# First key tiles row by row from smaller first transfers, the first weight unit in halves, ten products over a zeroed tile ahead of them

## The reference, cut to what matters

```python
def reference(x, mem, ..., mem_2, ...):
    x = first_block(x, mem, ...)          # recurrences, cross attention over mem, feed-forward
    return second_block(x, mem_2, ...)    # two layers more

def cross_attention(h, m, w_q, w_kv, w_o):
    q = (h @ w_q).reshape(...)
    kv = m @ w_kv                         # m = rms_norm(mem, norm_mem_g)
    k = kv[..., :D_MODEL].reshape(...)
    ...
```

## Time and profile before

| | us |
|---|---|
| time, median of 3 runs | 2022.88 |
| lowest, highest | 2019.67, 2024.22 |
| span of the profiled execution | 2016.9 |
| TensorE busy in it | 1983.3 |
| first product of TensorE | 9.50 |
| head of w1 begins | 37.80 |

### The profile page before, as it was taken

The page is one execution under the profiler, slowest core; times in us unless marked ns, Lnnn a source line. Parts: engine busy times, 40 slices in busy tenths (PEclk is TensorE's granted clock), DMA queues, the critical chain, the costliest instruction groups (busy, mean ns, idle before and its releaser), DMA issues.

```text
span 2016.9 us, 37724 instructions
## 1 busy us (share of the span) xinstructions
PE 1983.3 (98%) x15408; PEld 1848.6 (92%) x15408; DVE 1341.4 (67%) x1866; ACT 1082.0 (54%) x1698; POOL 51.8 (3%) x47
## 2 busy tenths in 40 slices
PE   8999999999999999999999999999999999999998
PEld 8989988999899989899988998999899989888997
DVE  6786766787566667866767554655477677756554
ACT  5856555555454454556556444644454565645443
POOL 0021000000000000000100000000000001000000
PEclk9999999999999999999999999999999999999999
DMA  7522454666565547543564655565555535544553
GB/s 274 172 80 76 151 184 157 209 207 196 173 221 190 199 166 231 183 136 127 199 209 143 209 189 191 189 208 194 194 198 185 178 107 189 180 162 168 189 191 122
DMA packets 98730, 359.30 MB, mean 178 GB/s; under 512 B 11193, under 2 KB 11513, under 8 KB 98297
## 3 DMA queue, kind: packets, MB, share of 16 engines
q1 hardware_dynamic: 98560, 356.90, 52.4%
HBM read 353.65 MB, written 1.05 MB: 176 GB/s over the span
## 4 chain that ended last, share of the span: by engine, by line
PE 92%; ACT 3%; DVE 3%; issue 1%; DMA 0%; DVEq 0%; SPq 0%; ACTq 0%
PE ps L1039 17%; PE ps L1041 17%; PE ps L1040 17%; PE ps L1026 8%; PE ps L1115 7%; PE ps L1114 7%; PE ps L1113 7%; PE ps L1195 2%; PE ps L1080 2%; PE ps L1081 2%; PE ps L1082 2%; PE ps L1196 2%; PE ps L1202 2%; ACT whi L2462 1%; DVE wlo L1718 1%; ACT Xn L2466 1%
## 5 line engine op out<-in xcount | busy, mean ns | idle before, releaser
L1718 DVE TENSOR_TENSOR wlo<-raw,whi 128x1024 fp32r<-128x1024 f32 x635 | 773.1, 1227 | 462.4 <-ACT whi L2462 460.3
L2462 ACT ACTIVATE whi<-raw 128x1024 fp32r<-128x1024 f32 x635 | 664.6, 1056 | 353.8 <-PE ps L1115 154.4
L1039 PE MATMUL ps<-H,whi 128*128 128x256 f32 x2608 | 734.1, 281 | 2.5 <-DVE wlo L1718 1.8
L1040 PE MATMUL ps<-L,whi 128*128 128x256 f32 x2608 | 725.4, 278 | 0.0
L1041 PE MATMUL ps<-H,wlo 128*128 128x256 f32 x2608 | 725.4, 278 | 0.0
L1039 PEld LDWEIGHTS ps<-H,whi 128*128 128x128 f32 x2608 | 490.1, 188 | 8.5 <-issue 4.2
L1040 PEld LDWEIGHTS ps<-L,whi 128*128 128x128 f32 x2608 | 490.2, 188 | 0.6
L1041 PEld LDWEIGHTS ps<-H,wlo 128*128 128x128 f32 x2608 | 490.1, 188 | 0.0
L1113 PE MATMUL ps<-whi,HH 128*128 128x512 f32 x440 | 171.2, 389 | 0.0
L1114 PE MATMUL ps<-whi,HL 128*128 128x512 f32 x440 | 171.2, 389 | 0.0
L1115 PE MATMUL ps<-wlo,HH 128*128 128x512 f32 x440 | 171.2, 389 | 0.0
(11 more groups left out here) (439 smaller groups left out, 2938.6 us busy)
## 6 DMA issues: line engine op xcount, KB each, us to landing
raw<-in_ws SPq DMA_DIRECT2D x635, 512.0 KB, 3.8
prow<-in_rows SPq DMA_DIRECT2D x11, 512.0 KB, 5.8
row<-in_rows SPq DMA_DIRECT2D x9, 512.0 KB, 6.4
mema<-in_memT SPq DMA_DIRECT2D x4, 512.0 KB, 4.8
mema<-in_mem2T SPq DMA_DIRECT2D x4, 512.0 KB, 6.8
memb<-in_mem2T SPq DMA_DIRECT2D x4, 512.0 KB, 5.8
DT<-in_dec SPq DMA_DIRECT2D x2, 768.0 KB, 6.5
X<-in_x SPq DMA_DIRECT2D x1, 1024.0 KB, 10.7
```

Of the source, the lines that this page charges most:

```text
L1039: e.matmul(o, h, hs[k], start=first and k == 0, stop=False, skip_group_check=True)
L1040: e.matmul(o, h, ls[k], start=False, stop=False, skip_group_check=True)
L1718: e.tensor_tensor(m.wlo[:, n % SPL, :], r, h.bitcast(F32), SUB).then_inc(*c.lo.done(n))
L2462: e.activation(m.whi[:, n % SPL, :], m.raw[:, n % RAW, :], ACT.Copy).then_inc(*c.hi.done(n))
```

## The change

The first transfers become smaller and come in another order: a quarter of `mem`, the 8 columns of `vec` with its gain, the first half of weight unit 0, its second half, the next quarter, unit 1, two quarters, units 2 and 3; then the rest of `vec` in two pieces, and `cst`, X, unit 4 and `prow` as before. Unit 0 is split in two halves. Key tiles 0 to 3 are made together, two rows of `mem` at a time over all four tiles (`first_keys`), so that unit n holds rows 2n and 2n+1 of four tiles. GpSimd zeroes 256 columns of `rx`, and TensorE makes ten plain float32 products of 128 columns over them into a bank that nobody reads. Of the steps that follow, `keys` 4 and 5 now both stand ahead of `mem_added`, `keys_out` 0 to 2 and the transposes, `keys` 6 and 7 behind them; both `jn` stand behind all of key tiles 0 to 3.

```diff
@@ key_fillers
-        if n == 3 and i == 0:
-            steps += [("mem_added", 0)] + mem_sums(0) + [("keys_out", i, 0), ("keys_out", i, 1)]
-        elif n % 2 and (n > 3 or i):
+        if n % 2:
             steps.append(("keys_out", i, n // 2))
@@ order
     o.put("first")
-    for step in mem_pieces(0):
+    pieces = mem_pieces(0)
+    for step in pieces[:4]:
         o.put(*step)
-    o.fill.append(key_fillers(0)[1:])
-    o.work("keys", 0, 0)
+    for part, some in enumerate((pieces[4:6], pieces[6:7], pieces[7:], ())):
+        o.put("first_keys", part)
+        for step in some:
+            o.put(*step)
     o.put("jn", "x0", 0)
     o.put("jn", "x0", 1)
-    o.filler(4)
+    o.put("keys", 0, 4)
+    o.put("keys", 0, 5)
+    o.put("mem_added", 0)
+    for step in mem_sums(0):
+        o.put(*step)
+    for p in range(3):
+        o.put("keys_out", 0, p)
     for tb in range(2):
         o.put("jt", "x0", tb)
         o.put("jh", "x0", tb, 0)
         o.put("jh", "x0", tb, 1)
-    o.filler(10 ** 6)
+    o.put("keys", 0, 6)
+    o.put("keys", 0, 7)
+    o.put("keys_out", 0, 3)
@@ tensor_program
+    def first():
+        bank = bank_for("warm")
+        e.wait_ge(*pool.after("warm"))
+        for _ in range(WARM):          # 10
+            mm = e.matmul(bank[:, 0:128], m.rx[:, 0:128], m.rx[:, 128:256], start=True, stop=True, ...)
+        mm.then_inc(*pe.done(("warm",)))
+
+    def first_keys(part):
+        mem, mh, ml = m.mem(0)
+        if part == 0:
+            for j in range(2):
+                bank_for("keys", 0, j, hold=True)
+        for k in (2 * part, 2 * part + 1):
...
+            if part == 0:
+                e.wait_ge(*(c.hi.sem, 1) if k else act.after("first_hi"))
+            for n, i in rows:
...
+                e.matmul(o, m.weight(i)[0], mh[:, k, :], ...)
+            if part == 0:
+                e.wait_ge(*(c.lo.sem, 1) if k else dve.after("first_lo"))
+            for n, i in rows:
...
+                e.matmul(o, m.weight(i)[1], mh[:, k, :], ...)
+            e.wait_ge(*dve.after("ml", 0, k))
+            for n, i in rows:
...
+                mm = e.matmul(o, m.weight(i)[0], ml[:, k, :], ...)
@@ vector_program, mem; scalar_program the same with first_half, second_half and first_halves(p + 1)
                 if i == t == 0:
-                    remainders(1)
+                    first_remainder()
+                elif i == 0 and t == 1:
+                    second_remainder()
...
+        if i == 0 and p < 4:
+            remainders(p + 1)
         if i == 0 and p == 3:
-            remainders(3)
+            e.wait_ge(c.land["vec"], 32)
@@ pool_program, first
+        e.memset(m.rx[:, 0:256], 0.0).then_inc(*pool.done(("warm",)))
@@ sync_program, first
-        e.dma_start(m.vec[:, :], ins["vec"]).then_inc(c.land["vec"], 16)
-        memory(0, 0)
-        units(1)
-        memory(0, 1)
+        a = VEC_AT["norm_mem_g"][0]
+        first_memory(0)
+        e.dma_start(m.vec[:, a:a + 8], ins["vec"][:, a:a + 8]).then_inc(c.land["gain"], 16)
+        e.dma_start(m.raw[:, 0, 0:512], ins["ws"][0, :, 0:512]).then_inc(c.land["first"], 16)
+        e.dma_start(m.raw[:, 0, 512:1024], ins["ws"][0, :, 512:1024]).then_inc(c.land["raw", 0], 16)
+        loaded[0] = 1
+        first_memory(1)
+        units(2)
+        first_memory(2)
+        first_memory(3)
         units(4)
+        for to, of in ((0, a), (a + 8, NV)):
+            e.dma_start(m.vec[:, to:of], ins["vec"][:, to:of]).then_inc(c.land["vec"], 16)
```

More of the change, by code:

```diff
@@ L24 @@
 NU = 635
+WARM = 10
 C_W = math.exp(-0.5)
@@ L1265, in keys @@
              [dve.after("ml", i, t) for t in range(8)], quarters or (0, 4))
+    def first():
+        bank = bank_for("warm")
+        e.wait_ge(*pool.after("warm"))
+        for _ in range(WARM):
+            mm = e.matmul(bank[:, 0:128], m.rx[:, 0:128], m.rx[:, 128:256], start=True, stop=True, skip_group_check=True)
+        mm.then_inc(*pe.done(("warm",)))
[5 more added lines that the diff above has]
+        for k in (2 * part, 2 * part + 1):
+            rows = []
+            for n in range(4):
+                spec = full("w_ckv", 0, k, 128 * n)
+                if part:
+                    rows.append((n, tile(*spec)))
+                else:
+                    rows.append((n, len(plan)))
+                    plan.append(spec)
+            if part == 0:
+                e.wait_ge(*(c.hi.sem, 1) if k else act.after("first_hi"))
+            for n, i in rows:
+                o = banks.of("keys", 0, n // 2)[:, (n % 2) * T:(n % 2 + 1) * T]
+                if n == 0:
+                    e.wait_ge(*act.after("mh", 0, k))
+                e.matmul(o, m.weight(i)[0], mh[:, k, :], start=k == 0 and n % 2 == 0, stop=False, skip_group_check=True)
+            if part == 0:
+                e.wait_ge(*(c.lo.sem, 1) if k else dve.after("first_lo"))
+            for n, i in rows:
+                o = banks.of("keys", 0, n // 2)[:, (n % 2) * T:(n % 2 + 1) * T]
+                e.matmul(o, m.weight(i)[1], mh[:, k, :], start=False, stop=False, skip_group_check=True)
+            e.wait_ge(*dve.after("ml", 0, k))
+            for n, i in rows:
+                o = banks.of("keys", 0, n // 2)[:, (n % 2) * T:(n % 2 + 1) * T]
+                mm = e.matmul(o, m.weight(i)[0], ml[:, k, :], start=False, stop=k == 7, skip_group_check=True)
+                names = [("keys", 0, n)] * (k == 7) + [("unit", i // UT)] * (i % UT == UT - 1)
+                if names:
+                    mm.then_inc(*pe.done(*names))
+        if part == 3:
+            for j in range(2):
+                banks.release("keys", 0, j)
     def mem_rms(i):
@@ L1681, in branch_ready @@
         return [dve.after("yl", l, n, k // 2) for k in range(4)]
-    run = {"out_row": out_row, "tail": tail, "jt": turned_row, "head": head, "begin": begin, "go_on": go_on, "hidden_turned": hidden_turned, "keys": keys, "values": values, "mem_added": mem_added, "w1": w1,
+    run = {"first": first, "first_keys": first_keys, "out_row": out_row, "tail": tail, "jt": turned_row, "head": head, "begin": begin, "go_on": go_on, "hidden_turned": hidden_turned, "keys": keys, "values": values, "mem_added": mem_added, "w1": w1,
            "kn": kn, "lora_up": lora_up, "px": in_tile("px", 14), "py": in_tile("py", 18), "gate1": in_tile("gate1", 22),
@@ L1743, in first, with first_remainder, second_remainder @@
     def first():
-        e.wait_ge(c.land["vec"], 16)
+        e.wait_ge(c.land["gain"], 16)
+    def first_remainder():
+        h, r = m.whi[:, 0, 0:512], m.raw[:, 0, 0:512]
+        e.wait_ge(*act.after("first_hi"))
+        tt(m.wlo[:, 0, 0:512], r, h.bitcast(F32), SUB, ("first_lo",))
+    def second_remainder():
+        h, r = m.whi[:, 0, 512:1024], m.raw[:, 0, 512:1024]
+        e.wait_ge(c.hi.sem, 1)
+        e.tensor_tensor(m.wlo[:, 0, 512:1024], r, h.bitcast(F32), SUB).then_inc(*c.lo.done(0))
+        split[0] = 1
     def mem(i, p):
@@ L2478, in first, with first_half, second_half @@
         do(m.scr[:, 0:1], m.scr[:, 7:8], ACT.Sqrt)
-        e.wait_ge(c.land["vec"], 16)
+        e.wait_ge(c.land["gain"], 16)
+    def first_half():
+        e.wait_ge(c.land["first"], 16)
+        do(m.whi[:, 0, 0:512], m.raw[:, 0, 0:512], ACT.Copy, ("first_hi",))
+    def second_half():
+        e.wait_ge(c.land["raw", 0], 16)
+        e.activation(m.whi[:, 0, 512:1024], m.raw[:, 0, 512:1024], ACT.Copy).then_inc(*c.hi.done(0))
+        split[0] = 1
     def mem(i, p):
@@ L2486, in mem @@
         if p < 4:
-            e.wait_ge(c.land["mem", i, p // 2], 16)
+            e.wait_ge(c.land["mem", i, p if i == 0 else p // 2], 16)
             for t in (2 * p, 2 * p + 1):
@@ L2490, in mem @@
                 if i == t == 0:
-                    first_halves(1)
+                    first_half()
+                elif i == 0 and t == 1:
+                    second_half()
         elif p < 6:
@@ L2496, in mem @@
             do(MEM[:, t:t + 4, :], MEM[:, t:t + 4, :], ACT.Square, ("mem_sq", i, p))
+        if i == 0 and p < 4:
+            first_halves(p + 1)
         if i == 0 and p == 3:
-            first_halves(3)
+            e.wait_ge(c.land["vec"], 32)
     def root(name, divisor, bias=0, mult=1.0):
@@ L3043, in memory, with first_memory @@
         e.dma_start(flat(m.mem(i)[0][:, :, :])[:, s], ins[mem_of(i)[0]][:, s]).then_inc(c.land["mem", i, h], 16)
+    def first_memory(q):
+        s = slice(2 * q * T, 2 * (q + 1) * T)
+        e.dma_start(flat(m.mem(0)[0][:, :, :])[:, s], ins["memT"][:, s]).then_inc(c.land["mem", 0, q], 16)
     def first():
-        e.dma_start(m.vec[:, :], ins["vec"]).then_inc(c.land["vec"], 16)
-        memory(0, 0)
-        units(1)
-        memory(0, 1)
+        a = VEC_AT["norm_mem_g"][0]
[8 more added lines that the diff above has]
+        first_memory(3)
         units(4)
+        for to, of in ((0, a), (a + 8, NV)):
+            e.dma_start(m.vec[:, to:of], ins["vec"][:, to:of]).then_inc(c.land["vec"], 16)
```

(4 more changed lines are left out.)

## The result

The changed kernel takes 2026.80 us (median of 20 executions, 2022.88 to 2029.27), the kernel before 2021.36 us (20 executions, 2017.46 to 2026.50). The ratio is 1.0024, with a 95% interval of 1.0017 to 1.0031: slower by 0.24%, or 3.4 to 6.3 us. The forecast was 2026.7 us, and that it is met to 0.1 us is luck: by the medians the change costs 5.4 us where 3.8 were forecast, and the base of the forecast, the median of the three executions known then, was 1.5 us above that of the twenty. The two errors cancel. The profiled execution of the changed kernel took 2029.25 us by its own time, its span is 2027.2 us.

The account below looks back on a forecast made before the run. TensorE, busy 1983.3 of 2016.9 us, bounds the kernel, with VectorE's chain to `K` deciding the start. 4.6 (later `K`) - 2.9 (fewer key tiles behind) + 2.1 (clock) = 3.8 us on 2022.88 gives 2026.7 us, range 2021.0 to 2030.0.

Parts of the forecast that it names:

- The banks and the wait for K: At the last four transposes of the start, TensorE would wait 5 us for VectorE's `K`, where before it waited 0.3.
- VectorE's chain: VectorE from unit 4's remainder at 18.2 us to the first `K` at 33.36: 15.16 us, ending 4.6 us later.
- The landing of unit 4: In SyncE's queue, the same bytes ahead: unit 4 lands as before at 16.8 us, up to 1 later; 17.1 taken.
- rival C: Smaller first transfers move slowly; unit 4 lands at 17.8 to 18 us, another +0.8 us, 2027.5 us; chance 0.18.
- The two key tiles in place of three: On TensorE behind the wait for `K`, two key tiles are left where before it was three: 2.9 us less.
- The clock: TensorE's clock falls to the lower level in the wait for `K`, costing 1.5 to 2.6 us; 2.1 taken.
- The sum: Over the kernel's start: 4.6 - 2.9 + 2.1 = 3.8 us more, so 2026.7 us.
- The start: First products near 6 us, unit 1 landed near 8.2, key tiles 0 to 3 ended near 19.1; head start about 4.4.
- The chances: For the whole kernel's time: within 0.2% 0.56, slower by more 0.39, faster by more 0.05.
- The likeliest case: At the start, `K` comes later and the clock falls: 2026.7 us, range 2025 to 2028.5, chance 0.52.

Follow-up runs that it names:

- Old transfers: The changed kernel with all first transfers as before (`vec` whole and first, `mem` in halves, unit 0 whole); ratio 1.0023.
- reordered change: The changed kernel with the transfers of before, both sums ahead of remainder 4, and sums over channels, reciprocal and two `keys_out` ahead of key tiles 4 and 5; ratio 0.9998.
- sums first: The changed kernel with both of VectorE's sums of squares ahead of the remainders of units 4 and 5; ratio 1.0015.
- before with products: The kernel before with 22 plain products over a zeroed tile added ahead of its first key product; ratio 0.9975.
- sums on GpSimd: The kernel before with 22 plain products added at the start and VectorE's two sums replaced by three additions on GpSimd; ratio 1.0.
- clock held: The changed kernel with 20 plain products put into TensorE's wait for `K`, ahead of the next to last four transposes; ratio 1.001.

## Why the prediction held, and where it was off

**The banks and the wait for K.** Right: 4.62 us of waiting where 5 was written, in the last four transposes, ended by `K`.

**VectorE's chain.** Right to 0.1 us: 15.16 us were summed, 35.06 - 19.91 = 15.15 measured. Remainder 5, 6, 7 and 8 and both sums stand where they were put, and ScalarE was ahead at each.

**The landing of unit 4.** Mis-sized: 17.1 taken from bounds of 16.8 to 17.8, 18.7 measured. That is rival C's effect, slow first transfers, with twice its price: 1.95 us. Its reason, that SyncE needs 0.45 us to issue each, isn't borne out: by 5 us SyncE was 1.7 MB ahead of what was moved. Old transfers in the changed kernel give 16.7. The step that failed is "the same bytes stand ahead of unit 4, so it lands as before": bytes alone didn't set it.

**The two key tiles in place of three.** Nearly right: -2.9 written. With the clock held up the head follows K by 6.41 us, before by 9.03, so -2.6.

**The clock.** Right that it falls. Taken at 2.1, measured at 2.16 by holding it up; but 2.1 was a midway value, and five other executions lost 1.1 to 1.5 us, so that it is met this closely is luck. In the change it was low for 6.8 us, of which 5.3 lay behind the wait. The rule of the Trainium skill in "TensorE: Matmul & The Clock Gate", under HAM oscillation, that waits for data between groups of products bring the array back to the slow clock, agrees with this trace: a wait of 4.62 us, then products 0.21 us apart. For shorter waits the rows go both ways: the clock fell behind 1.73 us in the reordered change, and stayed up behind 1.42 us in sums first and behind 1.70 us without work in before with products. Among waits this short the length alone doesn't decide it.

**The sum.** 4.6 - 2.9 + 2.1 = 3.8 was written; the profiles give (35.06 - 28.77) - 2.62 + 2.16 = 6.29 - 2.62 + 2.16 = 5.83 us. Of the 2.03 missing K is 1.7, which is the landing but for 0.05, and the two key tiles are 0.3. The medians say 3.4 to 6.3.

**The start.** Products began earlier as said, and it was worth nothing. The wait for unit 1 was worse than written (landed at 10.0 and not 8.2, a wait of 3.58 us and the clock low again from 13.1 to 16.5 us), with the same slow transfers, and the four key tiles ended at 22.5 us and not at 19.1. TensorE had those microseconds to spare: it still came to the wait 4.62 us before K.

**The chances.** The interval of the ratio lies around the 0.2% bound that divides "same" (0.56) from "slower" (0.39), and its middle is on the slower side. The likeliest case was the right one; C, at 0.18, happened along with it.

## What to carry to other kernels

An engine that is busy for 98% can still be bound by another for its first 30 us: follow each engine's queue in order up to the first result that frees a buffer, and count the buffers. A head start is worth what the slowest queue to that point lets through, and an in-order queue makes the place of an instruction that must wait for a transfer part of the price: put what is ready ahead of it. Here smaller first transfers brought the first products from 9.50 to 5.42 us and the fifth unit from 16.8 to 18.7; both have to be costed. And when a forecast is met, look at its terms: here errors of 1.5 and 1.6 us cancelled.

## What the hardware showed that was not expected

**First transfers.** With the same bytes ahead of it, a unit landed at 16.7 to 17.4 us behind 9 transfers (eight programs) and at 18.2 to 19.2 behind 14 (four). Between 5 and 7 us the queue moved 111 to 161 GB/s in place of 365 to 393, which is worth 1.2 us by the amount; the rest has no cause shown. With either half of the small ones undone it landed at 17.6 and 17.7.

**VectorE beside GpSimd.** During GpSimd's additions in float32, VectorE's subtraction over 128 x 1024 took 2.59 us in place of 1.2 (sums on GpSimd).

**TensorE's pace at a granted clock of 1.00.** The part of the two spans' difference that isn't the change's lies here (the same work, 7 us shifted; kernel before first, the change second):

```profile
600.00:640.00 40.00, 40.00 (x356) 40.00 (x355) 26.02 (x36) 18.39 (x22) 0.00 (x0) 1.00 0.63 201
640.00:680.00 40.00, 40.00 (x356) 40.00 (x355) 26.91 (x35) 19.21 (x23) 0.00 (x0) 1.00 0.59 192
```

```profile
607.00:647.00 40.00, 40.00 (x342) 40.00 (x341) 25.44 (x35) 18.02 (x21) 0.00 (x0) 1.00 0.63 196
647.00:687.00 40.00, 40.00 (x342) 40.00 (x342) 25.91 (x36) 18.59 (x23) 0.00 (x0) 1.00 0.56 180
```

356 products in 40 us are one per 0.112 us, 342 one per 0.117, TensorE never idle and the clock granted in full in both. In the profiles the pace belongs to a stage: a main loop of a feed-forward (100 to 140 us, some 130 the one here) runs at one of the two from its first product to its last, with one exception (clock held, which changes near 400 us), and which of the two changes from execution to execution of nearly the same program, for 4 to 5 us a stage. What decides it at the start of a stage was not found. It goes with the span: there are five such loops, and the five profiles in which three of them have the faster pace span 2016.5 to 2021.7 us, the nine others 2023.2 to 2027.9. So it is probably the largest part of why executions of one kernel spread by up to 0.8%, and why ratios of some ten executions can't tell 2 us.
